# Two unused buffers that move the large SBUF buffers of both ends onto multiples of 512 bytes

## What is computed

```python
def peer(xn, w_q, sub_keys, u, v):
    q = (xt @ w_q).reshape(T, PEER_HEADS, 2, PEER_HALF)
    s = jnp.einsum('thpc,hpnc->thpn', q, sub_keys)
    s1, i1 = lax.top_k(s[:, :, 0], PEER_TOPK)
    s2, i2 = lax.top_k(s[:, :, 1], PEER_TOPK)
    ...                       # the 16 best of 16 x 16 pairs: expert, gate
    h = jax.nn.gelu(jnp.einsum('cd,chkd->chk', xc, u[ec]), approximate=False)
    return jnp.einsum('chk,chkd->cd', gc * h, v[ec])

for l in range(DEPTH):        # DEPTH = 2
    ...                       # layer 0: differential attention; layer 1: dilated attention
    x = x + jnp.concatenate([mix, mo], axis=-1) @ w_out[l]
    x = x + peer(rmsnorm(x, norm_ffn[l]), peer_wq[l], peer_keys[l], peer_u[l], peer_v[l])
return rmsnorm(x, final_norm)
```

## The kernel before

| buffers | side | start past a multiple of 512 bytes, before | after |
|---|---|---|---|
| `x`, `ident`, `masks` | left | 128 | 128 |
| `front_raw`, `front_w`, `front_mem` (odd small buffers ahead of them) | left | 0 | 64 |
| `a_in_h` (input of the attention of layer 0) | right | 480 | 0 |
| `ma_w`, `ma_wv`, all large `ma` | left | 448 | 0 |
| `o0_w` | left | 448 | 0 |
| layer 0: `peer_x`, `peer_raw`, `peer_hi`, `peer_lo` | right | 480 | 0 |
| layer 0: `p_w_raw`, `p_g_sb`, `p_w_hi`, `p_w_lo`, `p_grow`, `p_acc` | left | 448 | 0 |
| `dil_h`, `sv`, large `ba` | left | 448 | 0 |
| layer 1: `mem_kT`, `mem_v`, `o` | right | 480 | 0 |
| layer 1: `peer_x`, ring, `o1_w`, `p_w...`, `p_grow` | left | 448 | 0 |

## Time and profile before

### The profile page before, as it was taken

One profiled execution on the slowest core, in us unless ns is written; L12 is line 12 of the kernel. 1 busy time (PEld: TensorE's weight loads), 2 busy tenths in 40 slices (PEclk: granted clock), 3 DMA queues, 4 the chain that ended last, 5 costly groups with the idle time before them and its releaser, 6 DMA issues. The chain is left out here.

```text
span 3454.4 us, 49213 instructions
## 1 busy us (share of the span) xinstructions
PE 3285.0 (95%) x18534; PEld 2920.1 (85%) x18534; DVE 2666.9 (77%) x5415; ACT 1400.3 (41%) x2205; POOL 1126.0 (33%) x666
## 2 busy tenths in 40 slices
PE   7988999999999999998999998999999999999997
PEld 6866899999998788886978876799989998788886
DVE  4664799898976888885457875699898976788886
ACT  3333245545453333332435544234545453333332
POOL 1311363423312464450000001354342422466561
PEclk9988999999999999999999998999999999999999
DMA  4102358878889999993222212348888789999995
GB/s 163 62 7 91 123 170 294 290 268 292 274 315 345 389 389 388 379 384 133 96 74 74 74 44 80 122 131 287 286 272 283 274 312 338 392 391 390 388 390 204
DMA packets 324349, 833.65 MB, mean 241 GB/s; under 512 B 26001, under 2 KB 160657, under 8 KB 320017
## 3 DMA queue, kind: packets, MB, share of 16 engines
q1 hardware_dynamic: 250384, 562.04, 46.3%
q0 software_dynamic: 73728, 268.47, 21.4%
HBM read 721.30 MB, written 109.10 MB: 240 GB/s over the span
## 5 line engine op out<-in xcount | busy, mean ns | idle before, releaser
L1959 ACT ACTIVATE peer_hi<-peer_raw 128x1024 fp32r<-128x1024 f32 x540 | 570.5, 1057 | 651.9 <-PE p_bank L1933 358.6
L2173 DVE TENSOR_TENSOR peer_lo<-peer_raw,peer_hi 128x1024 fp32r<-128x1024 f32 x434 | 532.3, 1227 | 339.4 <-ACT peer_hi L1959 339.1
L1862 POOL DMA_INDIRECT p_grow<-in_u_rows,p_expert x256 | 329.6, 1287 | 758.4 <-DVE p_hid L2181 744.3
L1862 POOL DMA_INDIRECT p_grow<-in_v_rows,p_expert x256 | 452.3, 1767 | 362.9 <-DVE p_acc L2190 315.0
L1933 PE MATMUL p_bank<-peer_hi,p_w_hi 128*128 128x512 f32 x1536 | 478.4, 393 | 3.7 <-DVE peer_lo L2173 3.6
L1933 PE MATMUL p_bank<-peer_lo,p_w_hi 128*128 128x512 f32 x1536 | 478.5, 393 | 0.0
L1933 PE MATMUL p_bank<-peer_hi,p_w_lo 128*128 128x512 f32 x1536 | 478.2, 392 | 0.0
L1884 PE MATMUL p0r_h_ps<-peer_x_hi,peer_hi 128*128 128x384 f32 (+1 forms) x1152 | 401.9, 349 | 11.9 <-ACT p_h_sb L1973 6.6
L1884 PE MATMUL p1r_h_ps<-peer_x_hi,peer_hi 128*128 128x384 f32 (+1 forms) x1152 | 401.3, 348 | 10.0 <-ACT p_h_sb L1973 6.5
L1884 PE MATMUL p0r_h_ps<-peer_x_lo,peer_hi 128*128 128x384 f32 (+1 forms) x1152 | 395.4, 343 | 0.0
L1884 PE MATMUL p1r_h_ps<-peer_x_lo,peer_hi 128*128 128x384 f32 (+1 forms) x1152 | 395.1, 343 | 0.0
(11 more groups left out here) (365 smaller groups left out, 5806.5 us busy)
## 6 DMA issues: line engine op xcount, KB each, us to landing
peer_raw<-in_u SPq DMA_DIRECT2D x256, 512.0 KB, 5.0
peer_raw<-in_v SPq DMA_DIRECT2D x256, 512.0 KB, 10.6
hiddens<-p_h_sb SPq DMA_DIRECT2D x256, 192.0 KB, 3.4
p_w_raw<-hiddens SPq DMA_DIRECT2D x64, 768.0 KB, 10.1
p_g_sb<-gates SPq DMA_DIRECT2D x64, 768.0 KB, 14.0
gates<-x SPq DMA_DIRECT2D x12, 2048.0 KB, 9.5
ba_w<-in_w_b_mix SPq DMA_DIRECT2D x38, 512.0 KB, 3.7
peer_raw<-in_w_peer_q SPq DMA_DIRECT2D x32, 512.0 KB, 4.0
```

Of the source, the lines that this page charges most:

```text
L1862: pool.indirect_dma_start(out=grow[:, g % RG, :], out_offset=None, in_=table, in_offset=bass.IndirectOffsetOnAxis(ap=expert[:, at:at + 1], ...
L1959: act.activation(hi[:, n % NH, :], raw[:, n % NR, :], ACT.Copy).then_inc(hi_ready, 1)
L2173: dve.tensor_tensor(lo[:, m % NH, :], raw[:, m % NR, :], hi[:, m % NH, :].bitcast(F32), ALU.subtract).then_inc(lo_dve, 1)
```

## The change

Two buffers are allocated that no instruction uses. `left_pad` takes 64 bytes a partition after the last of the small permanent buffers at the left end: everything allocated on the left afterwards lies 64 bytes higher. `right_pad` takes 480 bytes at the right end before anything else is put there: everything on the right lies 480 bytes lower. The offsets that come out stand in the last column of the table above. No instruction is added, removed or moved, and all sizes, waits and orders stay as they are.

```diff
@@ -2299,6 +2299,8 @@
         subln = sb("subln", [P, 2])
         rstd = sb("rstd", [P, TT])
         neg_lam = sb("neg_lam", [P, 1])
+        sb("left_pad", [P, 16])
+        ctx.enter_context(nc.sbuf_tensor("right_pad", [P, 120], F32, side="right"))
 
         x_dram = nc.dram_tensor("stream", (P, TT, D), F32).ap()
         g_dram = nc.dram_tensor("gates", (P, NTD, NK + 2, TB), F32).ap()
```

## The result

| | before | after |
|---|---|---|
| median, runs side by side | 3460.12 us (6 runs) | 3426.65 us (6 runs, 3423.70 to 3433.02) |
| ratio | | 0.9905, 95% interval 0.9887 to 0.9923 |
| span of the profiled execution | 3454.4 us | 3421.9 us |

The change is faster by 0.95%, 33.5 us. The runs of the kernel before that were made later lie near 3460 us (3458.5 to 3461.3 as medians of four further series), so its first median, 3453.63, was a low draw. Measured by the gain, 33.5 us against 14.2, the forecast is off by 19 us, more than the 12.7 us between the two medians, 3439.4 and 3426.65.

What follows compares the result with a forecast made beforehand. TensorE, busy 95% of the span, was taken as the bound, slowed in layer 0 by operands 32 bytes apart. Gains of 11.8 + 1.7 + 0.7 = 14.2 us took 3453.63 to 3439.4 us, range 3430 to 3448.

Steps and rivals of the forecast that it cites:

- Step (1): Value part of layer 0: matching operand offsets save 6.6 ns a matmul; 11.8 us gained, bounds 11.8 to 15.2.
- Step (2): `ma`: 336 matmuls of L1109 go from 0.2336 to 0.2275 us each; 1.7 us gained.
- Step (3): `o0`: 192 matmuls each 6.1 ns quicker; 0.7 us gained, bounds 0 and 1.2.
- Step (4): Pairs that match already, moved to offset 0: neither better nor worse, judged from `front`; 0 us.
- Step (5): Element-wise work on ScalarE and VectorE at offset 0: taken as 0, with 3.8 us at most either way.
- Step (6): Big loads landing on other offsets: taken as 0; TensorE waits for them only at two stops, 1.06 + 2.56 us.
- rival B: Loads to offset 0 land sooner and both value parts' stops go: 23.0 us gained, 3430.6 us; 17%.
- A: Offsets aren't the cause; operands in distant regions slow layer 0, so pads change nothing: 3453.6 us; 13%.
- C: Operands both at 0 collide like a 32-byte mismatch, so matching pairs lose 6.6 ns: +27 us, 3481; 5%.

Runs made afterwards that it cites:

- 448/448: Right pad of 32 bytes alone, against the kernel before: both ends' large buffers at 448; 3441.27 us, ratio 0.9949.
- 480/480: Left pad of 32 bytes and no right pad, against the kernel before: all large buffers at 480; 3444.23 us beside 3461.26, ratio 0.995.
- 128/128: Pads of 192 and 352 bytes, against the kernel before: both ends' large buffers at 128 past a multiple of 512; 3442.32 us beside 3458.53.
- 256/256: Left pad 320 bytes, right pad 224, against the kernel before: all large buffers at 256 past a multiple of 512; 3428.14 us, ratio 0.9915.
- 256 apart: Left pad 64 bytes, right pad 224, against the kernel before: left buffers at 0, right at 256; 3427.10 us beside 3461.26, ratio 0.9904.
- 128 and 64 apart: Two kernels against the one before, left buffers at 0: right ones at 384, 3446.62 us; right ones at 448, 3446.47 us.

## Why the prediction was wrong

**The stops tell most of it.** In the profiles, by layer: of the 8 value parts with all transfers off 256 and the quick pace in TensorE (448/448, 480/480 and 128/128, and layer 1 of before and of the right pad alone) every one has a stop of 1.97 us or more and takes 526.0 to 530.3 us. Of the 12 with aligned transfers and the quick pace (after twice, 256/256, 256 apart, and layer 1 of the left pad alone, of 128 and 64 apart and of `raw` moved in layer 0) one has, and the others take 522.0 to 523.0. With part of them aligned it is 3 of 7. A stop of 2 to 2.6 us adds some 4 us where the granted clock then falls to the lower level, and only its own length where it doesn't (524.7 us in the changed kernel's second profile, 524.8 with `raw` moved). The two value parts together take 1052.6 to 1054.6 us in the three matched kernels off 256 and 1044.6 to 1046.9 in the four profiles with all ends on it, some 8 us less.

**Step (1), the value part of layer 0: right in its mechanism, and in its size under its own premise.** The 6.6 ns of mismatch are there and go, as the 884 matmuls show. With transfers as they were, at 448, the part gained 12.1 us with the forecast's stop, 2.61 us idle at 55.9 us; forecast 11.8. In the changed kernel it gained 15.7. The sentence "the faster TensorE only waits longer" holds at 448. In the changed kernel it doesn't: it takes the landing of the loads as fixed, and the change moved that as well. One reading beside it is off: a granted clock of 0.83 over 10 us is 3.4 us at the lower level, half speed, which cost 1.7 us, and not 1.7 us at that level. The sum uses the cost, so it stands.

**Step (2), `ma`:** 0.8 us between first and last start, forecast 1.7; the other matched kernels gave 1.1 (448) to 2.3 (480). The pace fell from 232.9 to 228.7 ns over 336 matmuls, which is 1.4 us. **Step (3), `o0`:** 233.3 to 228.1 ns on 192 matmuls, 1.0 us, which can't be told apart in the stage, as the clock moves the stretch before it by more (below).

**Step (4), matching pairs at 0: right.** `front` at 256 columns was a sound witness for 512: 226.7 ns at 0, 256, 128, 448 and 480 alike, in the value parts. **Step (5), element-wise work: right.** The mean of `lo` on VectorE is 1226 ns after and 1227 before, and of `hi` on ScalarE 1058 and 1057. GpSimd's `lo` takes 2529 and 2542. So no quicker engine stands behind the second gain.

**Step (6), the transfers at 0: this is the step that failed.** It was put at nothing, though it named what quicker loads could remove: 1.06 + 2.56 us of stops and 1.7 of clock, 5.3 us, beside the 3.4 that step (1) had handed back (15.2 - 11.8). Together that is, but for rounding, rival B's 8.8, worked out and given 17%. The runs showed 11.4 us of median between matched ends at 448 and at 0 (one series) and 16.1 between 480 and 256 (another), with the stops nearly always gone. B's value parts were right: 522.5 us each forecast, 523.0 and 522.6 measured. The error was to take 387 and 389 GB/s at 448 and 480 alike for evidence against B. Both places are off 256; the trace of before has no large load on an aligned place in those parts, so it couldn't speak either way, and the sum should not have been carried by it. On this the Trainium skill, "DMA: Bandwidth & Descriptors", section "How a descriptor splits into AXI transactions", states that a piece must start at a 256-byte boundary. It speaks of what a piece reads, and here only the places written to in SBUF moved. The runs agree in where the line lies (256 yes; 128, 448, 480 no). They don't bear out the additional piece for long rows: with `raw` alone moved to 448, a block's row took 166.4 ns, as in the changed kernel.

**More than B.** B's 23.0 us would be 3430.6; measured were 33.5 us of gain. Of the runs' medians, matched ends alone gained 19.6, 17.0 and 16.2 us (448, 480, 128). Aligned ends gave another 11.4 (after beside 448, same series) to 17.1 (256 apart beside 480, same series), and 12.5 where no pair matched (left pad alone). The forecast's 14.2 us was thus also a little small for the matched ends: the profile at 448 is 20.0 us shorter than before, 12.1 of it in the value part of layer 0 and 1.1 in `ma`, and most of the rest in stretches that scatter.

Beyond the value parts' 20.0 us in the two profiles, 3.8 are the product parts. In layer 0 they take 733.5 to 734.4 us in the four profiles with all ends on 256 and 735.6 to 737.8 in the eight with a whole end off it. But the kernel with both ends at 448 and only the gates at 0 takes 733.8, and layer 1 has no such order: 733.7 with all at 448, 736.9 and 737.5 in two kernels whose loads there are all aligned (left pad alone, 64 apart). What makes the difference isn't settled.

Another 3.4 us is the end of `ma`, where the granted clock falls to the lower of its levels for a time. Windows of all engines, 220 to 280 us, of before, of after, and of the changed kernel's second profile:

```profile
220.00:280.00 60.00, 40.00 (x180) 28.31 (x179) 31.81 (x98) 22.88 (x56) 3.66 (x2) 0.64 0.14 47
```

```profile
220.00:280.00 60.00, 38.70 (x193) 28.70 (x192) 33.84 (x99) 25.15 (x59) 5.99 (x3) 0.74 0.19 62
```

```profile
220.00:280.00 60.00, 39.90 (x179) 28.33 (x179) 31.20 (x96) 23.20 (x57) 4.48 (x2) 0.63 0.15 52
```

0.64 before, 0.74 after, and 0.63 in the same changed kernel profiled again, with 52.6 us from `ma` to `o0` in the one and 56.1 in the other. This part of the difference between two profiles isn't the change's; the medians over several runs are what counts. `o1` has the same (66.9 before, 64.2 after, 67.0 in the second profile). Over all sixteen profiles the end of `ma` takes 52.5 to 57.3 us, `ba` to `o1` 353.1 to 360.3 and `o1` 64.0 to 67.3, without relation to the places.

**Rivals A and C** fell: A by the kernel at 448, C by 226.7 ns at 0 past 0. The sentence "which one is displaced doesn't matter" holds at 32 bytes and not at 64.

## What to carry to other kernels

Put large buffers on multiples of 256 bytes: it cost this kernel two pads of 64 and 480 bytes, and brought 11 to 17 us of 3460 by way of transfers and 16 to 20 by way of TensorE. Where two runs of the same matmuls differ by some ns at the same clock, look at where both operands start before anything else. And where the trace holds no case of the new condition (here, no aligned load in the busy part), two equal rows of the old one are no evidence that the new one will be equal: give the rival that rests on it more than 17%.

## What the hardware showed that wasn't expected

- TensorE, float32, 512 columns streamed past 128 loaded: 226.7 ns a matmul if both operands stand at the same offset within 256 bytes, 228.9 with 0 streamed past 448 loaded, 233.3 with 448 past 0, 232.4 at 128 apart, 233.3 at 32 apart either way.
- A load's cost hangs on the place of its destination: a 512-byte row took 27.1 ns at a multiple of 256 (27.0 to 27.3), 28.2 to 28.5 when only such rows were off it, and 30.4 to 30.8 when all loads were (128, 448, 480). Rows of 4096 bytes showed next to none of this by themselves: 166.4 ns for a block's row at 448 in layer 0, 165.6 and 166.4 in the two profiles of the changed kernel.
- Kinds of load that share the engines make each other's rows dearer: in layer 1 a block's row landing at 448 took 167.2 ns with the gates at 448 and 163.2 with the gates at 0. In the medians, moving either the gates or the rest off 256 cost 3 to 8 us of 3430, not clear of noise one by one, and moving both 11 to 17.
